# Thirteen products of a constant matrix on TensorE ahead of the first transposes: left out

## What is computed

```python
D_MODEL, SEQ = 1024, 512
h = rmsnorm(x, norm_g[l])                         # x * rsqrt(mean(x*x) + EPS) * g
(a_q, a_k, a_v, a_z, i_q, i_k, i_w, b_q, b_k, b_v, b_z, b_o, b_i, b_f, g_a, g_b) = \
    jnp.split(h @ w_in[l], offsets, axis=-1)
...
o_a = dsa_attention(q_a, k_a, v_a, q_i, k_i, w_i, k_sel)   # top-k sparse attention
y_a = (o_a * jax.nn.silu(a_z)) @ w_branch_a[l]
...
y_b = (h_b * jax.nn.silu(b_z)) @ w_branch_b[l]             # gated linear recurrence
merged = jax.nn.sigmoid(g_a) * y_a + jax.nn.sigmoid(g_b) * y_b
x = x + merged @ w_out[l]
return rmsnorm(x, final_norm_g)
```

## Time and profile before

| | |
|---|---|
| median of 3 runs | 498.1 us (497.74 to 498.28) |
| the profiled execution | 497.84 us |
| its span, first to last instruction | 495.8 us |
| TensorE's matmul row, busy | 486.3 us, 98% of the span |
| mean granted clock of TensorE | 0.997 |

### The profile page before, as it was taken

How to read it: one execution, slowest core, us unless ns; L and a number is a source line. 1 busy time by engine, 2 the same in 40 slices (tenths; PEclk the granted TensorE clock), 3 DMA queues, 4 the chain that set the end, 5 groups by cost and what they waited for, 6 DMA issues and landing times.

```text
span 495.8 us, 6585 instructions
## 1 busy us (share of the span) xinstructions
PE 486.3 (98%) x2370; PEld 401.5 (81%) x2370; DVE 254.6 (51%) x557; ACT 242.9 (49%) x443; POOL 237.9 (48%) x152
## 2 busy tenths in 40 slices
PE   7999999999999999999999999999999999999995
PEld 6788888888888888888877877888888888887885
DVE  3775778866999986517754555320111011135433
ACT  6876754544534885545666853512331233241422
POOL 4767131375557773256387452426643564362000
PEclk9999999999999999999999999999999999999998
DMA  8654422422242253122122134134314435352111
GB/s 285 201 150 130 134 86 78 107 86 80 68 129 86 85 149 85 44 65 71 44 78 68 52 97 106 51 98 129 80 50 125 127 88 181 115 177 121 42 61 67
DMA packets 45672, 50.52 MB, mean 102 GB/s; under 512 B 5220, under 2 KB 30468, under 8 KB 45576
## 3 DMA queue, kind: packets, MB, share of 16 engines
q1 hardware_dynamic: 43944, 47.65, 32.7%
q10 hardware_dynamic: 1696, 2.45, 1.7%
HBM read 47.44 MB, written 2.12 MB: 100 GB/s over the span
## 4 chain that ended last, share of the span: by engine, by line
PE 97%; DMA 1%; DVE 1%; ACT 0%; issue 0%; SPq 0%; DVEq 0%; ACTq 0%
PE pj L1658 24%; PE pj L1660 24%; PE pj L1659 24%; PE ob L1788 2%; PE tr L1780 2%; PE qb L1725 2%; PE qb L1724 2%; PE ob L1660 1%; PE qb L1660 1%; PE ob L1658 1%; PE qb L1658 1%; PE ob L1659 1%; PE qb L1659 1%; DMA x_tok<-in_x 1%; PE qb L1773 1%; PE qb L1772 1%
## 5 line engine op out<-in xcount | busy, mean ns | idle before, releaser
L583 POOL TENSOR_TENSOR w_lo<-w_raw,w_hi 128x1024 fp32r<-128x1024 f32 (+1 forms) x70 | 167.9, 2411 | 117.9 <-ACT w_hi L986 117.7
L1658 PE MATMUL pj<-h_hi,w_hi 128*128 128x512 f32 x288 | 113.0, 392 | 0.0
L1659 PE MATMUL pj<-h_lo,w_hi 128*128 128x512 f32 x288 | 112.4, 390 | 0.0
L1660 PE MATMUL pj<-h_hi,w_lo 128*128 128x512 f32 x288 | 112.3, 390 | 0.0
L986 ACT ACTIVATE w_hi<-w_raw 128x1024 fp32r<-128x1024 f32 x71 | 72.9, 1050 | 7.4 <-DMA w_raw<-in_w_out 6.2
L1658 PE MATMUL pj<-w_hi,h_hi 128*128 128x512 f32 x168 | 68.0, 405 | 0.0
L1660 PE MATMUL pj<-w_hi,h_lo 128*128 128x512 f32 x168 | 65.8, 392 | 0.0
L1659 PE MATMUL pj<-w_lo,h_hi 128*128 128x512 f32 x168 | 65.7, 391 | 0.0
L1660 PEld LDWEIGHTS pj<-h_hi,w_lo 128*128 128x128 f32 x288 | 54.1, 188 | 11.6
L1658 PEld LDWEIGHTS pj<-h_hi,w_hi 128*128 128x128 f32 x288 | 54.1, 188 | 10.5 <-issue 0.2
L1659 PEld LDWEIGHTS pj<-h_lo,w_hi 128*128 128x128 f32 x288 | 54.1, 188 | 9.9
(11 more groups left out here) (255 smaller groups left out, 862.7 us busy)
## 6 DMA issues: line engine op xcount, KB each, us to landing
w_raw<-in_w_in SPq DMA_DIRECT2D x59, 512.0 KB, 3.6
w_raw<-in_w_out SPq DMA_DIRECT2D x5, 512.0 KB, 3.7
x_tok<-in_x SPq DMA_DIRECT2D x4, 512.0 KB, 5.1
w_raw<-in_w_branch_a SPq DMA_DIRECT2D x8, 256.0 KB, 2.8
w_raw<-in_w_branch_b SPq DMA_DIRECT2D x8, 256.0 KB, 3.1
x_again<-in_x SPq DMA_DIRECT2D x1, 2048.0 KB, 9.4
w_late<-in_w_out SPq DMA_DIRECT2D x3, 512.0 KB, 6.9
out<-y_norm SPq DMA_DIRECT2D x4, 320.0 KB, 2.4
```

The source lines that it names most:

```text
L583: eng.tensor_tensor(lo[:, 0:m], raw_slot(n)[:, 0:m], hi[:, 0:m].bitcast(F32), ALU.subtract).then_inc(lo_by_dve if n in DVE_SLOTS else lo_b ...
L1658: pe.matmul(bank, a_hi, b_hi, start=first, stop=False)
L1659: pe.matmul(bank, a_hi, b_lo, start=False, stop=False)
L1660: return pe.matmul(bank, a_lo, b_hi, start=False, stop=last)
```

## The change

The thirteen products are left out, with their constant. The wait for pool_step ahead of them and the wait for the identity behind them stay. Nothing is put in their place.

```diff
@@ -77,7 +77,6 @@
 
 POOL_ROUNDS = (0, 1)
 LAG = 2
-WARM = 13
 DVE_SLOTS = (3, OUT0 + 2, OUT0 + 4, OUT0 + 6, OUT0 + 7)
...
             pe.wait_ge(pool_step, 2)
-            for _ in range(WARM):
-                pe.matmul(pj[1][:, 0:P], mask0, mask0, start=True, stop=True)
             pe.wait_ge(const_in, 32)
             for j in range(TILES):
                 pe.wait_ge(x_scaled, j + 1)
```

## The result

The changed kernel takes 499.57 us, the median of 9 runs (498.71 to 500.34), beside 497.99 for the kernel before in 9 runs (497.58 to 498.36). The ratio is 1.0033, with a 95% interval of 1.0025 to 1.0042: slower by 1.6 us. The forecast was 499.2 in 498.3 to 502.0.

A forecast was written before the change was run, and what follows sets the result against it. TensorE was taken to bound the kernel, busy for 98% of the span with no gap to catch up; 497.84 + 1.1 = 498.94 us for the profiled execution, with 0.26 to the median 499.2, range 498.3 to 502.0.

The forecast's parts named there:

- A: Forecast case: the clock rises among the transposes of x or just behind; +0.55 to +1.6 us, middle 499.2; chance 0.67.
- (1): At TensorE's start: removing the products' 26 records gains nothing directly, since TensorE's next work waits for VectorE's x_norm.
- rival D: At the start: without the products' reads x lands 0.23 us sooner, if transposes keep pace; faster, 497.9 us; chance 0.02.
- (2): The transposes of x on TensorE begin at the lower clock level: 0.213 us each instead of 0.109.
- (3): Transposes of x: if all 24 ahead of the fourth tile were cold, the loss is 1.6 us, the upper bound.
- (4): Clock rises 3.2 us after the first transpose or later: fourth tile 0.55 to 1.6 us late, 1.1 us taken.
- (5): From 11.19 us on, h_hi, h_lo, products, weight rounding and loads move by the same amount; nothing new is waited for.
- B: Transposes of x do not raise the clock, so the projections begin cold: 501.3 to 502.9 us, middle 502.1; chance 0.20.
- C: Not slower: the fourth tile's start stays set by its x_norm at 10.70 us; 498.1 us; chance 0.11.

The follow-up runs named there:

- e4: The changed kernel run again unchanged, for a second profile: 499.92 us, ratio 1.0047.
- e5: The changed kernel with ScalarE's copy of the first unit into stage put ahead of rounding the second weight slot (slot 6): 498.82 us, ratio 1.0019.
- e6: The kernel before with ScalarE's copy of the first unit into stage put ahead of rounding the second weight slot: 497.81 us, ratio 0.9998.
- the delayed kernel: The kernel before with 11 more products behind the wait for the first scaled tile, delaying the transposes at full clock: 500.03, 500.04 and 500.32 us, ratio 1.0048.
- e1: The kernel before with its 13 products at the start replaced by 26 transposes of a permutation matrix: 498.18 us, ratio 1.0006.
- e11: The changed kernel with slot 7's load issued only when slot 6's has landed: 499.26 us, ratio 1.0027.
- e7: The kernel before with 18 products at the start instead of 13: 498.43 us, ratio 1.0012.
- e3: The kernel before with 6 products at the start instead of 13: 499.09, 499.10, 499.44 and 500.18 us, ratio 1.0034.

## Why the prediction was right, and where it was short

Direction and range were right, and the mechanism was right for about 1.0 of the 1.6 us. The rest came from a wait that the prediction had ruled out. That 499.57 still lies within A's own 498.4 to 499.9 is in part luck: the clock's term was near its middle and left room for the missing one. Another batch of the same kernel came out at 499.92 (e4).

- (1) No gain from the work removed: right. x_norm is ready at the same time, and the DMA moves 396 GB/s from 3.0 to 6.1 us with no product running, as with them. That ends rival D.
- (2) 0.213 us for a cold transpose: right to the digit.
- (3) and (4) The fourth tile late by 0.55 to 1.6 us, 1.1 in the middle: the term measures 1.0 us as a median (e5 less e6). In the profiles it is 1.25 to 1.78 us. No profile of transposes alone had the rise 3.2 us after the first, the lower end of the range; it came after 4.3 to 6.0. The 1.6 was no strict bound: in e4 the first tile was 0.08 us later than in before and the second had a short gap, and the clock rose only when the fourth tile had begun.
- (5) "All move by the same amount; nothing new is waited for": this step failed. It is true of the order of work, but not of the loads' landing. TensorE's wait on stage appears in two of three profiles of the changed kernel, 0.8 us each, and in the delayed kernel. Taken out, it gives 0.9 us back in the changed kernel and 0.7 in the delayed one. The prediction had read "no gap" in the list of TensorE's waits as "no change", where stage came just in time behind a load whose landing varies by 1 us. The sum is 1.0 for the clock and 0.6 (1.58 - 1.0) to 0.9 for the wait.
- The rivals: B fell with e1, C with the profile (h_hi at 12.82 instead of 11.19), D with the DMA's rate.
- Two rows were misread, and nothing hangs on it: the pairs at 9.12 and 9.34 us in the earlier trace rows are the second tile's, not the third's, and from the product at 12.90 to the next it is 0.27 us; 0.23 is the step after that.

What stays open is whether the later start makes slot 6 land late, and how. In the five profiles with "small" within 0.1 us of 12.90 it landed after 4.7 to 5.4 us, in the seven later ones with slot 7's load behind it after 4.7 to 5.8: the ranges overlap, and only the later ones go past 5.4. Sharing with slot 7's load probably makes slot 6 late (e11), but in before and e4 the same two loads ran side by side and it landed after 4.7 us. The kernels e1 and e7, hardly late at all, also had 0.4 and 0.5 us of the wait. What decides how two loads share the DMA in one execution, no run here shows.

## What to carry to other kernels

Work without a use, put into time in which TensorE must wait anyway, is worth what the clock makes of the next work on the path, and it must last until the clock is up: here 13 products were enough and 6 were worth nothing. When you shift a kernel's start, look past the list of waits for places where a wait is just missed: an engine that works in order, with a wait for a load ahead of something the critical engine needs soon. Compare how soon the critical engine starts behind what it needs, where it waits and where it seems not to: with 0.15 us here and 0.14 there, nothing was left. A profile's single execution says whether such a wait happened, not how often it does; the same kernel profiled three times, and one run with the order changed, told that here.

## What the runs showed of the hardware

- Transposes alone raised TensorE's clock from its low level: 421 ns each until about 6.2 us, 272 after, 4.3 us after the first (e1).
- The time from the first work to the rise was not fixed: 3.3 us in before and some 5.5 in e6, both with products, and 4.3 to 6.0 in the profiles with transposes only. In e3, with 6 products and a pause of 2.9 us ahead, it rose 6.3 us after the first transpose.
- The granted clock's column read 1.00 over stretches in which the instructions' own durations show half the pace: before 4.2 us in the kernel before, and from 8 to 12 us in the changed kernel, where a transpose took 0.213 us.
- A load of 512 KB landed in 4.7 to 5.8 us with another of its size issued 0.4 us behind it (12 profiles), and in 4.6 with that one held back (e11, one profile).
- From the end of VectorE's work on stage to TensorE's start on it passed 0.14 to 0.15 us in each profile in which TensorE waited for it.
